# Preparing the second mixer's transposed input inside the first experts' last unit

## The reference, cut to what matters

```
h = h + ssd_memory_mixer(h, ...)                      # layer 0
h = h + hierarchical_moe(h, ...)                      # out_moe = sum over e of gates[:, e] * (he @ w_down[e])
k_sh, v_sh = shared_kv(h, kv_norm_w, w_kv, positions) # layer 1: rms_norm(h, kv_norm_w) @ w_kv
h = h + swa_memory_mixer(h, k_sh, v_sh, ...)          # rms_norm(h, b_norm_w) @ in_w
h = h + hierarchical_moe(h, ...)
return rms_norm(h, final_norm_w)
```

## Time and profile before

| | |
|---|---|
| Median of 3 runs | 1314.37 us (1312.51 to 1315.31) |
| The profiled execution, its own time | 1316.85 us |
| Its span, first to last instruction | 1314.9 us |
| Mean granted TensorE clock | 0.968 of 2.4 GHz |
| PE busy / DVE / ACT | 1197.8 / 280.6 / 205.3 us |
| Read from HBM | 460.91 MB, 351 GB/s over the span |

### The profile page before, as it was taken

How to read it: one execution, slowest core, us unless ns; L and a number is a source line. 1 busy time by engine, 2 the same in 40 slices (tenths; PEclk the granted TensorE clock), 3 DMA queues, 4 the chain that set the end, 5 groups by cost and what they waited for, 6 DMA issues and landing times.

```text
span 1314.9 us, 15025 instructions
## 1 busy us (share of the span) xinstructions
PE 1197.8 (91%) x5996; PEld 590.6 (45%) x5996; DVE 280.6 (21%) x679; ACT 205.3 (16%) x487; POOL 32.4 (2%) x42
## 2 busy tenths in 40 slices
PE   7999999999999999989687999999999999967695
PEld 5874765444344444533232465553344444422231
DVE  5741543031111111100000336231111111100001
ACT  2223323120000000000001335221000000000002
POOL 0001210000000000000000012000000000000000
PEclk9999989999999999998888999999999999987899
DMA  9930259589999999999999771689999999999997
GB/s 355 350 128 25 49 219 386 226 313 409 406 426 427 426 427 426 424 426 425 426 426 416 293 287 65 230 318 384 416 426 427 427 427 426 426 427 426 426 427 285
DMA packets 84728, 463.03 MB, mean 352 GB/s; under 512 B 7552, under 2 KB 9648, under 8 KB 36528
## 3 DMA queue, kind: packets, MB, share of 16 engines
q1 hardware_dynamic: 84656, 462.02, 85.6%
HBM read 460.91 MB, written 1.07 MB: 351 GB/s over the span
## 4 chain that ended last, share of the span: by engine, by line
PE 68%; SPq 16%; DMA 10%; DVE 2%; ACT 2%; issue 1%; DVEq 0%; ACTq 0%
PE bank L1590 19%; PE bank L419 14%; SPq L272 14%; PE bank L1599 10%; PE bank L1563 5%; DMA h<-in_w_down 5%; PE bank L1580 5%; PE bank L402 3%; PE bank L1918 2%; DMA h<-in_w_up 2%; DMA late<-in_w_down 2%; PE bank L358 1%; SPq L1359 1%; PE bank L387 1%; PE bank L1063 1%
## 5 line engine op out<-in xcount | busy, mean ns | idle before, releaser
L1590 PE MATMUL bank<-own,work 128*64 128x512 f32 (+1 forms) x1128 | 269.4, 618 | 20.1 <-DMA own<-in_w_up 9.8
L1590 PE MATMUL bank<-late,work 128*32 128x512 f32 (+1 forms) x560 | 144.2, 621 | 12.5 <-DMA own<-in_w_up 12.5
L1599 PE MATMUL bank<-own,work 128*32 128x512 f32 (+1 forms) x464 | 124.6, 657 | 27.2 <-DMA own<-in_w_down 11.3
L1590 PEld LDWEIGHTS bank<-own,work 128*64 128x64 f32 (+1 forms) x1128 | 77.4, 127 | 148.9 <-issue 148.8
L1468 DVE TENSOR_TENSOR work<-work,bank 128x512 f32<-128x512 f32 x24 | 25.5, 1061 | 474.9 <-ACT work L1527 474.9
L1563 PEld LDWEIGHTS bank<-work,xs 128*128 128x128 f32 x768 | 90.8, 194 | 39.9 <-issue 39.9
L1563 PE MATMUL bank<-work,xs 128*128 128x128 f32 x768 | 100.0, 284 | 2.1 <-DVE work L1400 2.1
L1527 ACT ACTIVATE work<-bank 128x512 f32<-128x512 f32 x24 | 14.3, 597 | 532.0 <-PE bank L1590 532.0
L1580 PE MATMUL bank<-work 128*128 128x512 f32 x192 | 87.1, 595 | 3.1 <-DVE work L1473 1.6
L419 PE MATMUL bank<-xnT,own 128*128 128x256 f32 x384 | 84.7, 380 | 0.0
L1599 PE MATMUL bank<-late,work 128*64 128x512 f32 (+1 forms) x232 | 70.6, 726 | 9.4 <-DMA own<-in_w_down 4.2
(11 more groups left out here) (324 smaller groups left out, 1304.7 us busy)
## 6 DMA issues: line engine op xcount, KB each, us to landing
own<-in_w_up SPq DMA_DIRECT2D x78, 1024.0 KB, 26.1
own<-in_w_gate SPq DMA_DIRECT2D x63, 1024.0 KB, 25.5
own<-in_w_down SPq DMA_DIRECT2D x54, 1024.0 KB, 26.4
late<-in_w_gate SPq DMA_DIRECT2D x38, 1024.0 KB, 25.7
late<-in_w_up SPq DMA_DIRECT2D x32, 1024.0 KB, 26.3
late<-in_w_down SPq DMA_DIRECT2D x28, 1024.0 KB, 25.7
own<-in_a_in_w SPq DMA_DIRECT2D x17, 1024.0 KB, 13.5
h<-in_w_down SPq DMA_DIRECT2D x10, 1024.0 KB, 28.5
```

The lines of the kernel that those rows point to most:

```text
L1590: ins = pe.matmul(bank[q * T:(q + 1) * T, :], self.xg[:, at:at + T], cut(tile(q), k=4)[:, k, :], start=(half == 0 and k == 0), stop=(half ...
L1599: ins = pe.matmul(self.b_down[out][q * T:(q + 1) * T, :], self.turned[:, at:at + T], cut(tile(q), j=2)[:, j, 512 * out:512 * out + 512], s ...
```

## The change

Before the last unit of layer 0 the sum banks already hold all of `h` but this unit's part. The new kernel copies them to `c.h` there (L1836 and L2045 of before, once more), transposes `c.h` into the gather and turn banks, and writes `xnT` and `xkT` from them. Before gate and up of the last unit PE waits for all of it. The last unit's own part is then added transposed: for each of the eight blocks of 128 columns PE makes one matmul of the block of `y` by the transposed gates (`delta`, four ahead of each half's `scatter`), and DVE adds it to `xnT` and to `xkT` with one `scalar_tensor_tensor` each. The `xT` units of mixer B are gone; `c.h` is copied again there, as before. The last unit's experts can't use the slots `RES`, `XNT` and `EXTRA` any more, so its 24 jobs go round 19 slots instead of 22, and the first tiles of mixer B move from `own1` to `own4` on. The row factors of mixer B come ahead of its first copy. The bank numbers of layer 1's sums are changed so that they fit the new rotation, and `final_norm` waits on one semaphore instead of two.

```diff
             slot = free.pop(0)
-            if slot == MKV and layer == 0 and (job[0] == "mem" or job[2] >= SIDE[0]):
+            while layer == 0 and (slot == MKV and (job[0] == "mem" or job[2] >= SIDE[0])
+                                  or slot in EARLY and job[0] == "expert" and job[2] == NU - 1):
                 slot = free.pop(0)
...
+EARLY = [RES, XNT, EXTRA]
...
+    def delta_bank(self, k):
+        bank = (self.b_gather, self.b_turn, self.b_gate, self.b_up)[k // 2]
+        return bank[:, SEQ * (k % 2):SEQ * (k % 2) + SEQ]
...
+            def early_residual():
+                m = self.m
+                dve.wait_ge(c.mixer_cleared, 1)
+                dve.wait_ge(s["early_sums"], 1)
+                for q in (0, 2):
+                    dve.tensor_copy(*copy_h(c, 0, q)).then_inc(m["h_dve"], 1)
+                for i in range(4):
+                    dve.wait_ge(m["xT_ev"], 2 * i + 2)
+                    dve.tensor_tensor(cut(c.extra[:, :], k=KD)[:, 2 * i:2 * i + 2, :], cut((self.b_gather, self.b_turn)[i % 2], k=2),
+                                      spread_last(c.f("kv_norm", 2 * i, 2 * i + 2), SEQ), ALU.mult).then_inc(m["xk_dve"], 1)
+
+            def add_delta(into, norm, k):
+                x = cut(into[:, :], k=KD)[:, k, :]
+                return dve.scalar_tensor_tensor(out=x, in0=self.delta_bank(k), scalar=c.f(norm, k, k + 1), in1=x, op0=ALU.mult, op1=ALU.add)
+
+            def late_residual(half):
+                m = self.m
+                dve.wait_ge(s["side_done"], 2 * len(SIDE) + 4 + 4 * half + 4)
+                dve.wait_ge(m["xT_ev"], KD)
+                dve.wait_ge(m["xk_dve"], 4)
+                for k in range(4 * half, 4 * half + 4):
+                    add_delta(c.xnT, "b_norm", k).then_inc(m["xn_dve"], 1)
+                for k in range(4 * half, 4 * half + 4):
+                    add_delta(c.extra, "kv_norm", k).then_inc(m["xk_dve"], 1)
...
+                if early:
+                    late_residual(0)
                 dve.wait_ge(s["down_done"], u * 2 + 2)
                 dve.tensor_copy(self.y[1][:, :], self.b_down[1][:, :]).then_inc(s["y1_ready"], 1)
+                if early:
+                    late_residual(1)
...
+            def early_transposes():
+                m = self.m
+                for i in range(4):
+                    pe.wait_ge(m["h_dve" if i < 2 else "h_act"], 2)
+                    if i == 0:
+                        pe.wait_ge(m["h_act"], 2)
+                    if i >= 2:
+                        pe.wait_ge(m["xT_ev"], 2 * (i - 2) + 2)
+                        pe.wait_ge(m["xk_dve"], i - 1)
...
+            def delta(half, signal=None):
+                for k in range(4 * half, 4 * half + 4):
+                    ins = pe.matmul(self.delta_bank(k), self.y[half][:, P * (k % 4):P * (k % 4) + P], self.gates_T[:, 0:SEQ], start=True, stop=True)
...
             def unit(u):
                 T, last = UNITS_OF[u][2], u == NU - 1
+                early = last and layer == 0
+                if early:
+                    pe.wait_ge(s["xg_ready"], u * 2 + 2)
+                    early_transposes()
+                    pe.wait_ge(self.m["xT_ev"], KD)
+                    pe.wait_ge(self.m["xk_dve"], 4)
...
                             pe.wait_ge(s["gates_ready"], u + 1)
+                            if early:
+                                delta(0, s["side_done"])
                             scatter((0,)).then_inc(s["half_summed"], 1)
...
                 pe.wait_ge(s["y1_ready"], u + 1)
-                scatter((1,), s["scattered"] if last else None)
+                if early:
+                    delta(1, s["side_done"])
+                ins = scatter((1,), s["scattered"] if last else None)
+                if layer == 0 and u == NU - 2:
+                    ins.then_inc(s["early_sums"], 1)
```

More of the change, by code:

```diff
@@ L54 @@
 EXTRA, XNT, TAIL, RES, MKV, MEMT = range(OWN + LATE, SLOTS)
[L55 removed]
+SUMS = [[0, 3, 4, 7], [2, 4, 5, 7]]
 WORK = GRAN + 3328
@@ L1508, in body @@
                 dve.wait_ge(o["scattered"], n + 2)
+                if layer == 0:
+                    for k in range(KD):
+                        add_delta(c.xnT, "b_norm", k)
+                    for k in range(KD):
+                        ins = add_delta(c.extra, "kv_norm", k)
+                    ins.then_inc(o["added"], 1)
             dve.wait_ge(s["ordered"], self.ORDERED + 1)
@@ L1525, in _ @@
                                        ACT.Copy).then_inc(s["side_ev"], 1)
+                if layer == 0 and u == NU - 1:
+                    act.wait_ge(c.mixer_cleared, 1)
+                    act.wait_ge(s["early_sums"], 1)
+                    for q in (1, 3):
+                        act.activation(*copy_h(c, 0, q), ACT.Copy).then_inc(self.m["h_act"], 1)
+                    for k in range(KD):
+                        act.wait_ge(s["side_done"], 2 * len(SIDE) + k // 2 + 1)
+                        act.activation(cut(c.xnT, k=KD)[:, k, :], (self.b_gather, self.b_turn)[k // 2 % 2][:, SEQ * (k % 2):SEQ * (k % 2) + SEQ],
+                                       ACT.Copy, scale=c.f("b_norm", k, k + 1)).then_inc(self.m["xT_ev"], 1)
                 act.wait_ge(*self.released(("expert", layer, u, "up", 1, 0)))
@@ L1705, in body @@
                 pe.wait_ge(o["gates_ready"], n + 1)
+                if layer == 0:
+                    for half in range(2):
+                        delta(half)
                 scatter().then_inc(o["scattered"], 1)
-            self.over_rounds(pe, most, body)
+                if layer == 0:
+                    pe.wait_ge(o["added"], n + 1)
+            self.over_rounds(pe, most, body, (self.m["xk_dve"], 4 + KD) if layer == 0 else None)
         if layer == 0:
@@ L1773, in freed @@
                     "out": (s["h_new"], i + 1)}[kind]
-        U = Units(c, order, freed, holds, first=[b for b in range(NBANK) if b not in SUMS[0]])
+        gate, up, gather, turn = (b for b in range(NBANK) if b not in SUMS[0])
+        U = Units(c, order, freed, holds, first=[gather, turn, gate, up])
         R = Router(c, U, s, 1, xnT, routing)
@@ L1937, in _ @@
                     U.wait_free(pe, key)
-                if kind == "xT":
-                    pe.wait_ge(s["h_dve" if i < 2 else "h_act"], 2)
-                    transposes(c, pe, out, [cut(c.h, t=NT)[:, t, (2 * i + kk) * P:(2 * i + kk + 1) * P] for kk in range(2) for t in range(NT)])
-                elif kind in ("kv", "q"):
+                if kind in ("kv", "q"):
                     n = B0 + (1 if kind == "kv" else 2 * (i % 2))
@@ L2113, in final_norm @@
     s = c.sems("final", "act dve left right")
-    stored = [c.sem(f"stored{t}") for t in range(NT)]
+    stored = c.sem("stored")
     main = c.sems("main", Experts.MAIN)
@@ L2128, in _ @@
                 sp.dma_start(c.out[0, t * P:(t + 1) * P, 512 * half:512 * half + 512],
-                             y[:, t, 512 * half:512 * half + 512]).then_inc(stored[t], 16)
-        for t in range(NT):
-            sp.wait_ge(stored[t], 32)
+                             y[:, t, 512 * half:512 * half + 512]).then_inc(stored, 16)
+        sp.wait_ge(stored, 16 * 2 * NT)
     @block.scalar
```

85 lines of the change are left out of this document (45 added, 40 removed).

## The result

The kernel after took 1319.45 us (median of 20 runs, 1314.21 to 1320.92), the kernel before 1314.78 us beside it (20 runs). The ratio of the runs is 1.0024, 95% interval 1.0016 to 1.0031: slower by 3.1 us (2.1 to 4.1), where +1.3 was forecast. Put on the forecast's own median of before, the ratio gives 1314.37 x 1.0024 = 1317.5, inside the forecast range (1312.6 to 1318.3); the median of the 20 runs itself, 1319.45, lies above it. The medians differ by more than the ratio because the 20 runs after lie in two groups, 5 from 1314.2 to 1316.5 and 15 from 1317.9 to 1320.9. The profiled execution took 1319.93 us, 3.08 above that of before.

The account below looks back on a forecast made before the run. Weight loads set the pace up to the last unit's down product, then PE up to the queries. +1.7 us for the early stall and -0.3 at the seam gave +1.4, rounded to +1.3: 1315.7 us, range 1312.6 to 1318.3.

Parts of the forecast that it names:

- rival 1: Ahead of the last unit's down product: the clock falls a second time, +3.3 us in sum, 1317.7; chance 0.19.
- The early stall: Ahead of the last unit's gate product: PE waits for transposes and copies, gate 7.25 us later without a clock fall; +1.7 us.
- The clock: PE's clock falls in the early stretch, losing 2.2 us, and not again ahead of down; likeliest case, chance 0.42.
- The loads: Weight tiles of the last unit and mixer B with 19 slots: later issues cost DMA nothing, 0 us.
- The seam: From the last unit's end to mixer B's queries: `delta` adds 3.42 us, dropped copies and transposes save 3.72; -0.3 us.
- The additions: DVE at the seam: eight per half at 0.45 us each, holding `y[1]` by 0.2 us at most.
- The row factors: Ahead of the copy of mixer B's first queries: ready at Q + 6.5, half a microsecond of margin.
- Q: The start of mixer B's first queries on PE, claimed 1.71 us after the last scatter's start instead of 5.43.
- rival 3: PE's jump past the overflow rounds shows between scatter and queries: bounds 0 and 1.7 us, taken as 0; chance 0.06.
- Rivals 2 and 4: 2: no early clock fall, 1313.3 to 1314.8, chance 0.24; 4: real gain from mixer B's waits, below -2.6 us, chance 0.09.

Follow-up runs that it names:

- e1: The kernel after without PE's overflow rounds of layer 0, so with no jump between last scatter and queries; ratio to before 0.9999, 1314.33 us.
- e7: The kernel after measured again, its meant shift of 128 idle instructions missing from the built program; ratio to before 1.0007, 1317.09 us.
- e9: The kernel after with 120 more idle PE instructions (satisfied waits) in unit 10's last down product; ratio to before 1.0033, 1320.51 us.
- e6: The kernel after with PE's jump ahead of its wait for `y[1]`, last `delta` and scatter in both branches; ratio to before 1.0038, 1319.16 us.
- e8: The kernel after with `delta` left out of the overflow rounds, so their body is as short as before; ratio to before 1.0023, 1317.82 us.
- e3: The kernel before with only the slots of the kernel after; ratio to before 1.0006, 1316.96 us.
- e11: e4 with 120 more idle PE instructions, as in e9; ratio to before 0.9983, 1313.21 us.
- e4: The kernel after with the early transposes behind the last unit's first gate product; ratio to before 1.0021, 1318.09 us.
- e5: The kernel after with the changes of e4 and e6 together; ratio to before 1.0025, 1317.75 us.
- e10: The kernel before with 68 more idle PE instructions in unit 10's last down product; ratio to before 1.0022, 1318.39 us.
- e12: The kernel before with 180 more idle PE instructions, 90 in each of two narrow units ahead of the last; ratio to before 1.0001, 1314.54 us.

## Why the prediction was right and wrong

The direction was right and the time lies in the range, but by luck: +1.4 was put together from +1.7 and -0.3, and +3.1 came from +0.55 and +2.56. The upper end of the range was there for rival 1, a second fall of the clock, which did not come in the trace after. "Slower by over 0.2%", which came true (0.24%), had a chance of 0.22.

**The early stall, +1.7 forecast, +0.55 measured.** Each step came, but earlier. Against the landing as fixed point the gate product came 7.69 us later than before (676.84 - 706.62 against 670.55 - 708.02), where 7.95 was forecast. At half clock it lost 1.55 us (5.19 for 3.64), not 2.2, since part of the fall passed under waits and the clock was back at 680.01. So PE was ready for down 2.51 us behind its weights (709.13 against 706.62), where 3.7 was forecast. Down at full clock took 3.64, as argued.

**The clock.** It fell early and not ahead of down, in 2.92 us of waiting with 0.66 busy. But the argument that 2.95 us is too short for a fall was weak: in e1, e7 and e9 it fell there for 3.4 us, and in e6 and e8 it did not. e7 is the same program as after, byte for byte, so the second fall of rival 1 comes in some executions and not in others; its chance of 0.19 was not too high.

**The loads, 0 forecast, 0 seen.** As forecast, the fourth tile of down's first half waited after for this unit's first gate product (its end 682.03, the issue 682.09), and it landed at 706.62, ahead of PE. e3 confirms that the slots cost nothing that shows.

**The seam, -0.3 forecast, +2.56 measured. This is the step that failed.** Its parts: `delta` cost 1.8 us for four matmuls (722.09 to 723.92; forecast 1.71). The additions went 0.39 us apart (1.66 for four), faster than the 0.45 forecast, and did not hold `y[1]`. The row factors have hardly any margin: in e1, where nothing delays the queries, they are done at 731.26, 7.0 us after Q at 724.27 (forecast 6.5), and ACT's copy of the first queries starts at 731.40, not held. Where no jump stands in the way, the parts give what the sum gave: e1's queries start 1.72 us after its scatter, and the seam, measured as above, takes 12.87 us in e1 and 12.93 in e11 (722.09 - 709.16) against 13.02 before, -0.15 and -0.09 where -0.3 was forecast. The term that was mis-sized is **rival 3, the jump past the overflow rounds**: taken as 0, bounded at 1.7, weighed at 0.06; it took 2.55 (2.6 by e1 beside e7). The bound rested on this sentence of the working: "else the transposes would have come later". It was true of a jump from instruction 6762 to 7069 of that program, which took 0.37 us, and the change moved both to 6830 and 7169, where it took 5.92. SP's quarter of a microsecond was of another engine with another program.

**Rivals.** Rival 1 (3.3 us by a second fall) has nearly the right sum by the wrong road, as far as the trace after goes. Rivals 2 and 4 did not come; the nearest to a real gain is e11 with 0.17%.

**Which place stalls.** With a block start at 7145, as e8 and e10 show, and blocks of 256, the others near by start at 6889 and 7401. That sorts all twelve kernels with a jump into three kinds. The target lies two blocks behind the jump's own in after, e4, e5, e6 and e7 (jumps at 6803 to 6830, targets at 7166 to 7169): the jump itself takes 5.85 to 5.92 us. The target lies in the next block, but 8 instructions ahead of its end, in e8 and e10 (7137): the jump is short, and PE stands at the block's end. The target lies in the next block with 76 or more instructions left in before, e3, e9, e11 and e12 (7069, 7249, 7286, 7289): neither. This fits what the Trainium skill says, quoted with the suspect above, of the two blocks held and of fetching in order. The block start is worked out from two kernels and was not tested by moving the code one instruction at a time.

**What stays open.** Why e11 gains 2.3 us in the median when the seam explains 0.1 to 0.3: e12 shows that the pad isn't the reason, and e11's profiled execution is 4.4 us ahead of before's already at the first gate product of the experts (274.77 for 279.19), ahead of all edits, so it can't tell. And the median of e7 leaves the size of the change's cost uncertain between 0.1% and 0.3%: of the seven kernels with a gap of the jump's own six are slower than before clear of their intervals, and e7, 1.0007, is not; nor is it apart from e1.

## What to carry to other kernels

An edit moves every later instruction of its engine. Where an engine has a taken jump, look at the jump's own row, at the instructions behind its target and at the instruction packets in the DMA records, and when a kernel is slower for no reason that its edit gives, shift the code by some idle instructions before the idea is given up: here the place alone was worth 0.22%, as much as the change. A releaser named beside a wait proves nothing until that engine's own row ends with the wait. And short dependent bursts do better behind a long product that is ready than ahead of it: with the pad 0.9983 (e11) against 1.0033 (e9), though without it the times did not differ (e4 1.0021, after 1.0024).

## What the hardware showed that was not expected

**The jump's price has a clock of its own.** In all kernels with a gap of the jump's own PE resumes at a fixed time behind the last wait ahead of the jump, whatever it has still to do: after 728.35 - 722.09 = 6.26 us, e7 6.19, e4 6.20, e8 6.11, e5 6.12, e10 726.87 - 720.80 = 6.07, and e6, with the jump in another place, 723.15 - 716.98 = 6.17. The jump's row starts there too, within 0.06 us (after 722.15, e10 720.81, e6 717.00): the sequencer runs ahead of the matmuls. The instruction packet starts 3.5 to 3.6 us behind the same point (after: 725.67 - 722.09 = 3.58; e10: 724.41 - 720.80 = 3.61; e6: 720.49 - 716.98 = 3.51), itself takes 0.88 us, and PE resumes 2.4 to 2.7 us after its start. Before has such a packet as well, 3.57 us behind its wait (724.77 - 721.20), and PE goes on beside it; so a packet at the seam is no sign of a stall by itself. What is seen as a gap is what PE's queued work doesn't cover: 6.26 less 3.71 of `delta` and scatter after, 6.07 less 1.98 of scatter in e10, 6.17 less 1.92 of down in e6. That is why e6 failed: with only 1.92 us queued ahead of the jump it had less cover, not more. By this, a jump with over 6.3 us of queued work behind the last wait ahead of it should not show; that was not tried.

**A gap of 2.5 us can bring the clock down, or not.** It fell to 1.2 GHz inside the gap in e4, e5, e6, e8 and e10, and not in after and e7. In e4 (2.50 us of gap) it then took 8.75 us for the queries, in after (2.55) 7.10.
